# A hybrid decoder step on one core: 72 instead of 64 tokens weighed row by row, in 18 groups six tiles apart, with the two products of a group joined

## The chip, the cores and the metric

The kernel is one program on one core of a Trainium2 chip. The metric is the device time of one execution in microseconds. A profile is one more execution, taken by the hardware profiler; its times are counted from the start of its span. "PE" is TensorE (its weight loads are listed apart as "PEld"), "DVE" is VectorE, "ACT" is ScalarE, "POOL" is GpSimd and "SP" is SyncE, which does nothing here but issue DMAs.

## The reference, cut to what matters

One decoder layer runs on 288 tokens: 256 of a prompt and 8 x 4 of a decode batch. A first half (an input projection, a short gated convolution, sparse attention in three branches, merge gates, an output projection) is followed by an expert mixer, and that is where the change does most of its work:

```
s = einsum('nhcd,hckd->nhck', qq, sub_keys)      # 8 heads, 2 halves, 128 keys
top, sel = top_k(s1 + s2, 16)                    # 16 of 128 x 128 experts per head
g = softmax(top)
a = gelu(einsum('nd,nhkd->nhk', hx, u_tab[eidx]))
y = einsum('nhk,nhkd->nd', g * a, v_tab[eidx])   # 8 x 16 = 128 experts per token
```

`u_tab` and `v_tab` have 16384 rows of 1024 numbers. In the attention half, the cached keys and values of the compressed branch go through a small two-layer network (`compress`: sums over 32 positions, a gelu, a product with `w2`), and the prompt's queries read 15 compressed values each next to the selected and the window values.

## The kernel before

**The expert mixer as dense work.** Both tables are read whole, 512 KB a tile. There are 128 tiles of `u` and 128 tiles of `v`. Every float32 product is made of three products in a reduced form: the weights and the moving operand are each split into a high and a low part (`w_hi`, `w_lo` by ACT and DVE, one pair of buffers each), and high x high, high x low and low x high are summed.

- The *u stage* (`split_tile`, called for `E_U + j`, lines 2119 to 2134) makes the activations of 128 experts for all 288 tokens: 16 matmuls with `w_hi` (line 2128) and 8 with `w_lo` (line 2133) a tile, 288 columns each. ACT applies the gelu. Between tile 71 and tile 94 PE also makes, for four tokens a time, the matrix of gates from two one-hot matrices (`route`, line 2182), which DVE multiplies with the activations.
- The *v stage* (`value_tile`) multiplies each tile with the weighted activations of the `ND` dense tokens. The high and the low part of the moving operand lie side by side, so a tile is 8 matmuls of 2 x ND = 448 columns with `w_hi` (line 2208) and 8 of ND = 224 columns with `w_lo` (line 2215). For every tile ACT and DVE split the weights (lines 957, 1417) and the moving operand (`mov_high`, line 1020, and `mov_low_part`, line 1628).

**The last `NE` = 64 tokens by rows.** They take part in the u stage like the others, but not in the v stage. Each of them needs just 128 rows of `v_tab`. POOL gathers these rows with indirect DMAs: `gather_row(k, q)` (line 596) brings the half rows (512 numbers) of 128 experts for one token, 128 x 512 x 4 bytes, and `gather_value` (line 603) brings a token's 128 activations, 128 x 4 bytes, from a copy in memory (`act_kept`). A *group* is `GRP` = 4 tokens: 8 row gathers and 4 value gathers. A *unit* is one half of a group: `weigh_unit(k)` multiplies the rows of four tokens with their weights, in four matmuls of 512 columns that lie side by side in the array (32 weight columns each, line 2246), in full float32, of which the profile records two matmuls each. It adds into bank 6 for the first halves and into bank 7 for the second halves. There is one buffer of rows for each half.

**The order of the work.** Every queue is written out by hand, with semaphores between the engines. PE makes the first unit of group g before value tile `UNIT_TILES[g]` = 13 + 7g and the second one `LATER` = 3 tiles behind it. POOL refills a half's buffer once PE has used it (`rows_used`), and spreads its gathers over the tiles of the period by waiting for the tile count (`at_tile`). The ring of 4 slots of 512 KB, filled by SP, feeds the tables: a slot is loaded again when DVE has made its low part. All DMAs, SP's and POOL's, run on the same 16 DMA engines of the core.

**The attention half.** `comp_out(u)` is the product with `w2`; for the values of the paged caches it makes four products with 64 rows of output each, and one copy by ACT (line 850) takes the two blocks. `prompt_values(u)` sums, for each of four heads r in turn, one product with 16 rows (the compressed values, line 1977) and then 2 or 4 products with 128 rows (line 1981). It is called four times. The cached keys and values are loaded by POOL and SP with one DMA a page.

Of the kernel before, what the change touches and what calls it, by code (L numbers as in the profile page):

```python
# [20 lines left out]
NH, NG, R = 8, 2, 4  # L21
HD = 64
# [7 lines left out]
P = 128  # L30
# [17 lines left out]
NE = 64  # L48
ND = NT - NE
GROUPS = (ND - P) // GRP  # L50
EGROUPS = NE // GRP
UNIT_TILES = [13 + 7 * g for g in range(EGROUPS)]
LATER = 3
SUM_AT = UNIT_TILES[-1] + LATER + 2
STAGE = 4
# [50 lines left out]
UP0 = 17904  # L106
# [112 lines left out]
def program(nc, A, O):  # L219
    with ExitStack() as ctx:  # L220
# [315 lines left out]
        def _(pool):  # L536
# [81 lines left out]
            def at_unit(g, x):  # L618

                if g + 1 < EGROUPS:  # L620
                    gather_value(g + 1, x)

            for g in range(1, EGROUPS):
                T = UNIT_TILES[g - 1]
                if g >= 2:
                    pool.wait_ge(S["s_weights"], 2 + g - 1)
                pool.wait_ge(S["rows_used"], 2 * (g - 1) + 1)
                gather_row(2 * g, 0)
                at_tile(T + 1)
                gather_row(2 * g, 1)  # L630
                at_unit(g, 0)
                at_tile(T + 2)
                gather_row(2 * g, 2)
                at_unit(g, 1)
                at_tile(T + 3)
                gather_row(2 * g, 3)
                pool.wait_ge(S["rows_used"], 2 * (g - 1) + 2)
                gather_row(2 * g + 1, 0)
                at_unit(g, 2)
                at_tile(T + 5)  # L640
                gather_row(2 * g + 1, 1)
                at_unit(g, 3)
                at_tile(T + 6)
                gather_row(2 * g + 1, 2)
                gather_row(2 * g + 1, 3)


        @block.scalar
        def _(act):
# [162 lines left out]
            for u, (t, v) in enumerate(UNITS):  # L812
# [34 lines left out]
                if v == 0:  # L847
                    act.activation(kcn[0:n, t, :], ps[0:n, 5, 0:P], ACT.Copy).then_inc(S["cmp_copied"], 1)
                elif t < 4:
                    act.activation(vc[0:64, 2 * t:2 * t + 2, :], ps[0:64, 5, 0:256].rearrange("p (b c) -> p b c", b=2), ACT.Copy)\  # L850
                        .then_inc(S["cmp_copied"], 1)
                else:
                    act.activation(vc[0:16, 8, :], ps[0:16, 5, 0:P], ACT.Copy).then_inc(S["cmp_copied"], 1)
# [833 lines left out]
        def _(pe):  # L1687
# [175 lines left out]
            def comp_out(u):  # L1863

                t, v = UNITS[u]
                n = P if t < 4 else 16
                pe.wait_ge(S["hid_ready"], u + 1)
                if u:
                    pe.wait_ge(S["cmp_copied"], u)
                w2 = M("w2")[:, v * HD:(v + 1) * HD]  # L1870
                if v == 0 or t == 4:
                    for g in range(NG):
                        last = pe.matmul(ps[0:n, 5, g * HD:(g + 1) * HD], hid[:, g * n:(g + 1) * n], w2, start=True, stop=True)
                else:
                    for b in range(2):
                        for g in range(NG):
                            last = pe.matmul(ps[0:64, 5, b * P + g * HD:b * P + (g + 1) * HD], hid[:, g * P + b * 64:g * P + b * 64 + 64], w2,
                                             start=True, stop=True)
                last.then_inc(S["comp_out"], 1)
# [86 lines left out]
            def prompt_values(u):  # L1966
# [8 lines left out]
                for r in range(R):  # L1975
                    o = ps[:, 5, r * P:(r + 1) * P]
                    pe.matmul(o, vc[0:16, 8, :], pT[0:16, 2048 + r * P:2048 + (r + 1) * P], start=True, stop=False)
                    for br in range(2):
                        for kt in range(qt + 1):
                            x = (4 * br + r) * (qt + 1) + kt  # L1980
                            last = pe.matmul(o, vnew[:, kt, br * P:(br + 1) * P], pT[:, x * P:(x + 1) * P], start=False,
                                             stop=(br == 1 and kt == qt))
# [277 lines left out]
            for t in range(PK):  # L2260
# [5 lines left out]
                if t - LATER in UNIT_TILES:  # L2266
                    weigh_unit(2 * UNIT_TILES.index(t - LATER) + 1)
# [133 lines left out]
```

## Time and profile before

| | |
|---|---|
| Time, median of 3 runs | 1222.1 us (1221.54 to 1223.38) |
| The profiled execution's own time | 1216.64 us |
| Its span | 1214.9 us |
| PE busy | 1187.8 us, 98% of the span |
| DVE, ACT, POOL busy | 826.3, 614.3, 559.8 us |
| Moved by DMA | 263.67 MB, mean 217 GB/s |
| Granted PE clock, mean | 0.994 |

The profiled execution took 5.5 us less than the median of the runs. Its time goes 1.7 us beyond its span, for what lies before the first and behind the last instruction. A group of instructions in a view is named by its line, its engine, what it writes and reads; "x8" is the count, and a time in square brackets is how long the engine was idle before the group, with what ended it.

### The profile page before, as it was taken

What the parts mean: (1) busy time and instruction counts of PE and PEld (TensorE: products, weight loads), DVE (VectorE), ACT (ScalarE), POOL (GpSimd) and SP (SyncE); (2) the same over time, 40 slices, a digit from 0 to 9 for tenths busy, and PEclk for the clock granted to TensorE, in tenths of its full rate; (3) what the DMA queues carried; (4) which work ended last, traced back from release to release, by engine and by line L of the source; (5) the groups of instructions that cost most, each with busy time, mean ns of one, the idle gap of its engine ahead of it and who ended that gap; (6) DMA issues with size and microseconds to landing.
All of it is one profiled execution on the core that took longest, in us unless ns stands there. A gap on an engine that the chain in (4) does not pass through costs nothing.

```text
span 1214.9 us, 23500 instructions
## 1 busy us (share of the span) xinstructions
PE 1187.8 (98%) x8372; PEld 1091.5 (90%) x8372; DVE 826.3 (68%) x1517; ACT 614.3 (51%) x1181; POOL 559.8 (46%) x525
## 2 busy tenths in 40 slices
PE   7999899999999999999999999999999999999998
PEld 5688898977899999999999999999888888888887
DVE  6445465754686799999946765666766667666666
ACT  5423464532353454554557775444555555555554
POOL 3430234432000387877678775001355556665640
PEclk9999998999999999999999999999999999999999
DMA  8672758867665367777776556777888888788883
GB/s 329 208 216 64 108 162 250 265 209 255 206 234 172 105 182 171 165 177 177 182 176 143 132 144 185 261 257 235 307 274 289 290 291 284 272 297 287 293 293 134
DMA packets 144740, 263.67 MB, mean 217 GB/s; under 512 B 55536, under 2 KB 84272, under 8 KB 143920
## 3 DMA queue, kind: packets, MB, share of 16 engines
q1 hardware_dynamic: 100176, 207.29, 52.2%
q0 software_dynamic: 37184, 51.48, 17.1%
q10 hardware_dynamic: 7264, 3.40, 1.2%
q8 instruction: 67, 1.10, 0.4%
q14 instruction: 49, 0.40, 0.1%
HBM read 246.18 MB, written 20.09 MB: 219 GB/s over the span
## 4 chain that ended last, share of the span: by engine, by line
PE 85%; issue 5%; SPq 2%; POOLq 2%; DMA 2%; DVE 2%; POOL 1%; ACT 1%; ACTq 0%; DVEq 0%
PE ps L2128 26%; PE ps L2208 18%; PE ps L2133 13%; PE ps L2215 9%; PE ps L1692 5%; PE ps L2246 3%; PE ps L2182 2%; PE ps L1838 1%; POOLq L551 1%; PE ps L1712 1%; POOL arena L552 1%; PE ps L1719 1%; DMA xT<-in_xT 1%; DMA arena<-in_cache_cmp_v 1%; PE ps L2158 1%
## 5 line engine op out<-in xcount | busy, mean ns | idle before, releaser
L1417 DVE TENSOR_TENSOR w_lo<-ring,w_hi 128x1024 fp32r<-128x1024 f32 x271 | 331.6, 1224 | 130.5 <-ACT w_hi L957 112.0
L957 ACT ACTIVATE w_hi<-ring 128x1024 fp32r<-128x1024 f32 x280 | 294.9, 1053 | 203.8 <-issue 111.2
L2128 PE MATMUL ps<-h_hi,w_hi 128*128 128x288 f32 x1088 | 296.8, 300 | 0.5 <-ACT w_hi L957 0.5
L2128 PE MATMUL ps<-h_lo,w_hi 128*128 128x288 f32 x1024 | 277.7, 295 | 0.0
L587 POOL DMA_INDIRECT gates<-arena x128 | 237.4, 1855 | 67.2 <-issue 44.3
L2128 PEld LDWEIGHTS ps<-h_hi,w_hi 128*128 128x128 f32 x1088 | 205.0, 188 | 1.2 <-ACT w_hi L957 1.0
L2128 PEld LDWEIGHTS ps<-h_lo,w_hi 128*128 128x128 f32 x1024 | 192.6, 188 | 0.0
L596 POOL DMA_INDIRECT arena<-in_v,aux x128 | 131.4, 1027 | 129.9 <-PE ps L2215 59.2
L2133 PE MATMUL ps<-h_hi,w_lo 128*128 128x288 f32 x1088 | 166.8, 295 | 0.2 <-DVE w_lo L1417 0.2
L2133 PEld LDWEIGHTS ps<-h_hi,w_lo 128*128 128x128 f32 x1088 | 152.0, 188 | 0.5 <-DVE w_lo L1417 0.5
L2208 PE MATMUL ps<-h_hi,w_hi 128*128 128x448 f32 x512 | 118.2, 373 | 3.7 <-issue 2.9
L2208 PE MATMUL ps<-mov,w_hi 128*128 128x448 f32 x512 | 117.0, 370 | 0.6 <-issue 0.5
L2208 PEld LDWEIGHTS ps<-h_hi,w_hi 128*128 128x128 f32 x512 | 92.3, 190 | 23.9 <-issue 17.1
L603 POOL DMA_INDIRECT arena<-act_kept,aux x64 | 61.3, 957 | 111.7 <-DMA act_kept<-arena 92.5
L2208 PEld LDWEIGHTS ps<-mov,w_hi 128*128 128x128 f32 x512 | 91.4, 189 | 20.4 <-issue 14.1
L577 POOL TENSOR_TENSOR w_lo<-ring,w_hi 128x1024 fp32r<-128x1024 f32 x9 | 24.5, 2727 | 127.3 <-ACT w_hi L957 127.2
L1020 ACT ACTIVATE h_hi<-arena 128x448 fp32r<-128x448 f32 x64 | 37.0, 578 | 86.5 <-PE ps L2215 66.3
L1020 ACT ACTIVATE mov<-arena 128x448 fp32r<-128x448 f32 x64 | 37.0, 578 | 83.0 <-PE ps L2215 62.8
L2215 PEld LDWEIGHTS ps<-h_hi,w_lo 128*128 128x128 f32 x512 | 67.4, 192 | 1.9
L1628 DVE TENSOR_TENSOR h_hi<-arena,h_hi 128x448 fp32r<-128x448 f32 x64 | 40.0, 625 | 42.7 <-ACT h_hi L1020 26.3
L2215 PEld LDWEIGHTS ps<-mov,w_lo 128*128 128x128 f32 x512 | 67.1, 191 | 1.9
L1628 DVE TENSOR_TENSOR mov<-arena,mov 128x448 fp32r<-128x448 f32 x64 | 40.0, 626 | 40.5 <-ACT mov L1020 26.5
(361 smaller groups left out, 1975.4 us busy)
## 6 DMA issues: line engine op xcount, KB each, us to landing
ring<-in_uT SPq DMA_DIRECT2D x128, 512.0 KB
ring<-in_v SPq DMA_DIRECT2D x128, 512.0 KB
ring<-in_wout SPq DMA_DIRECT2D x32, 512.0 KB
ring<-in_wT SPq DMA_DIRECT2D x28, 512.0 KB
gates<-aux SPq DMA_DIRECT2D x32, 256.0 KB, 5.9
ring<-in_wtok SPq DMA_DIRECT2D x8, 512.0 KB
arena<-in_cache_slc_v POOLq DMA_DIRECT2D x64, 64.0 KB
act_kept<-arena SPq DMA_DIRECT2D x32, 128.0 KB
```

The costliest lines, as they stand in the source:

```text
L587: pool.indirect_dma_start(gates, bass.IndirectOffsetOnAxis(rt("gi")[:, P + s:P + s + 1].bitcast(U32), 0), rt("gi")[:, s:s + 1], None, comp ...
L596: pool.indirect_dma_start(e_rows[k % 2][:, 512 * q:512 * q + 512], None, A["v"].rearrange("t p (c f) -> (t p c) f", f=512), bass.IndirectO ...
L603: pool.indirect_dma_start(e_act[:, n:n + 1], None, act_kept, bass.IndirectOffsetOnAxis(act_list[:, ND + n:ND + n + 1], 0))\
L957: act.activation(w_hi[e % 2][:, :], ring[:, (W_O + e) % RING, :], ACT.Copy).then_inc(S["w_high"], 1)
L1020: act.activation(mov_parts[t % 2][:, :, 0, :], rows[:, 2 * pp:2 * pp + 2, :], ACT.Copy).then_inc(S["mov_high"], 1)
L1417: dve.tensor_tensor(w_lo[e % 2][:, :], ring[:, (W_O + e) % RING, :], w_hi[e % 2][:, :].bitcast(F32), ALU.subtract)\
L1628: dve.tensor_tensor(mov_parts[t % 2][:, :, 1, :], rows[:, 2 * pp:2 * pp + 2, :], mov_parts[t % 2][:, :, 0, :].bitcast(F32), ALU.subtract)\
L1692: last = pe.matmul(ps[:, bank, 0:NT], ring[:, i % RING, at + k * P:at + (k + 1) * P], rhs[:, k, :], start=(k == 0), stop=(k == n - 1))
L2128: last = pe.matmul(ps[:, bank, 0:NT], w_hi[e % 2][:, k * P:(k + 1) * P], mov[:, k, :], start=(k == 0 and mov is mov_hi), stop=False, skip_ ...
L2133: last = pe.matmul(ps[:, bank, 0:NT], w_lo[e % 2][:, k * P:(k + 1) * P], mov_hi[:, k, :], start=False, stop=(k == KC - 1), skip_group_chec ...
L2208: last = pe.matmul(ps[:, VBANK[dh][m], 0:2 * ND], w_hi[e % 2][:, h * 512 + m * P:h * 512 + (m + 1) * P], both[h], start=(t % HALF == 0 and ...
L2215: last = pe.matmul(ps[:, VBANK[dh][m], 0:ND], w_lo[e % 2][:, h * 512 + m * P:h * 512 + (m + 1) * P], both[h][:, 0:ND], start=False, stop=( ...
```

## The change

Five things change:

1. `NE` goes from 64 to 72 tokens by rows, so `ND` goes from 224 to 216. The dense groups that the route products make go from 24 to 22, the groups by rows from 16 to 18. `UNIT_TILES` is 13 + 6g (13 to 115) in place of 13 + 7g (13 to 118).
2. The two units of a group are made one behind the other, before the same tile; `LATER` is gone.
3. POOL's order in a period is new: both halves' buffers are refilled together. The old order in a period was (r a row gather, v a value gather, T the tile of the group): r, then at T+1 r v, at T+2 r v, at T+3 r, then (second half free) r v, at T+5 r v, at T+6 r r. The new one is r r r, at T+1 r r v, at T+2 r v v, at T+3 r r v.
4. `prompt_values` makes the four 16-row products first, then the others.
5. `comp_out` makes two products for all units, and ACT takes the paged values in two copies of 128 columns.

```diff
-NE = 64
+NE = 72
...
-UNIT_TILES = [13 + 7 * g for g in range(EGROUPS)]
-LATER = 3
-SUM_AT = UNIT_TILES[-1] + LATER + 2
+UNIT_TILES = [13 + 6 * g for g in range(EGROUPS)]
+SUM_AT = UNIT_TILES[-1] + 2
...
                 if g >= 2:
                     pool.wait_ge(S["s_weights"], 2 + g - 1)
-                pool.wait_ge(S["rows_used"], 2 * (g - 1) + 1)
-                gather_row(2 * g, 0)
+                for half in range(2):
+                    pool.wait_ge(S["rows_used"], 2 * (g - 1) + half + 1)
+                    gather_row(2 * g + half, 0)
+                gather_row(2 * g, 1)
                 at_tile(T + 1)
-                gather_row(2 * g, 1)
-                at_unit(g, 0)
+                gather_row(2 * g + 1, 1)
+                gather_row(2 * g, 2)
+                next_value(g, 0)
                 at_tile(T + 2)
-                gather_row(2 * g, 2)
-                at_unit(g, 1)
+                gather_row(2 * g + 1, 2)
+                next_value(g, 1)
+                next_value(g, 2)
                 at_tile(T + 3)
                 gather_row(2 * g, 3)
-                pool.wait_ge(S["rows_used"], 2 * (g - 1) + 2)
-                gather_row(2 * g + 1, 0)
-                at_unit(g, 2)
-                at_tile(T + 5)
-                gather_row(2 * g + 1, 1)
-                at_unit(g, 3)
-                at_tile(T + 6)
-                gather_row(2 * g + 1, 2)
                 gather_row(2 * g + 1, 3)
+                next_value(g, 3)
...
-                    act.activation(vc[0:64, 2 * t:2 * t + 2, :], ps[0:64, 5, 0:256].rearrange("p (b c) -> p b c", b=2), ACT.Copy)\
-                        .then_inc(S["cmp_copied"], 1)
+                    for b in range(2):
+                        last = act.activation(vc[0:64, 2 * t + b, :], ps[64 * b:64 * b + 64, 5, 0:P], ACT.Copy)
+                    last.then_inc(S["cmp_copied"], 1)
...
-                if v == 0 or t == 4:
-                    for g in range(NG):
-                        last = pe.matmul(ps[0:n, 5, g * HD:(g + 1) * HD], hid[:, g * n:(g + 1) * n], w2, start=True, stop=True)
-                else:
-                    for b in range(2):
-                        for g in range(NG):
-                            last = pe.matmul(ps[0:64, 5, b * P + g * HD:b * P + (g + 1) * HD], hid[:, g * P + b * 64:g * P + b * 64 + 64], w2,
-                                             start=True, stop=True)
+                for g in range(NG):
+                    last = pe.matmul(ps[0:n, 5, g * HD:(g + 1) * HD], hid[:, g * n:(g + 1) * n], w2, start=True, stop=True)
...
                 for r in range(R):
                     o = ps[:, 5, r * P:(r + 1) * P]
-                    pe.matmul(o, vc[0:16, 8, :], pT[0:16, 2048 + r * P:2048 + (r + 1) * P], start=True, stop=False)
+                    pe.matmul(o, vc[0:16, 8, :], pT[0:16, 2048 + r * P:2048 + (r + 1) * P], start=(r == 0), stop=False, skip_group_check=True)
+                for r in range(R):
+                    o = ps[:, 5, r * P:(r + 1) * P]
...
                 if t in UNIT_TILES:
                     weigh_unit(2 * UNIT_TILES.index(t))
-                if t - LATER in UNIT_TILES:
-                    weigh_unit(2 * UNIT_TILES.index(t - LATER) + 1)
+                    weigh_unit(2 * UNIT_TILES.index(t) + 1)
```

A place in the arena that depends on `ND` moves too (`UP0` 17904 to 17520).

## Rows read from the trace of the kernel before

**Rows 1.** The page: busy time of each engine, and the chain that ended last by line.
```profile
PE 1187.8 (98%) x8372; PEld 1091.5 (90%) x8372; DVE 826.3 (68%) x1517; ACT 614.3 (51%) x1181; POOL 559.8 (46%) x525
...
PE ps L2128 26%; PE ps L2208 18%; PE ps L2133 13%; PE ps L2215 9%; PE ps L1692 5%; PE ps L2246 3%; PE ps L2182 2%; PE ps L1838 1%; POOLq L551 1%; PE ps L1712 1%; POOL arena L552 1%; PE ps L1719 1%; DMA xT<-in_xT 1%; DMA arena<-in_cache_cmp_
```
**Rows 2.** Windows: a 7-tile period, then 860 to 868; last: clock, DMA share, GB/s.
```profile
960.45:980.46 20.01, 20.01 (x129) 17.24 (x129) 13.04 (x16) 10.70 (x14) 11.64 (x13) 1.00 0.84 290
...
860.00:864.00 4.00, 1.15 (x7) 0.87 (x5) 1.39 (x2) 1.52 (x2) 3.08 (x4) 0.94 0.96 378
864.00:868.00 4.00, 3.97 (x17) 3.50 (x16) 2.07 (x4) 1.89 (x3) 0.02 (x1) 0.64 1.02 408
```
**Rows 3.** The chain in order of time, v stage: start, us, what.
```profile
880.48 1.00 PE ps L2246 x8
881.48 1.84 PE ps L2208 x8
883.32 0.88 PE ps L2215 x8
884.20 1.63 PE ps L2208 x8
...
900.49 0.99 PE ps L2246 x8
```
**Rows 4.** The chain in order of time: matmuls of 512, 256, 34 and 288 columns.
```profile
21.55 1.85 PE ps L1712 x8
...
60.95 6.91 PE ps L1838 x32
...
109.37 3.66 PE ps L1838 x32
...
729.14 2.16 PE ps L2128 x16
...
733.25 2.16 PE ps L2128 x16
...
736.46 2.13 PE ps L2128 x16
```
**Rows 5.** Line 2246, the units: count, durations in ns, first and last start.
```profile
L2246 PE MATMUL ps<-arena x256: 592/605/617, 880.4 to 1191.1; 128*32 128x512 f32 x128
```
**Rows 6.** Timeline of POOL, v stage; in brackets the idle time before.
```profile
962.33 1.16 POOL L596 DMA_INDIRECT arena<-in_v,aux  x1 [1.84 <-PE ps L2246]
...
965.77 0.95 POOL L603 DMA_INDIRECT arena<-act_kept,aux  x1 [0.30 <-issue]
...
971.91 1.00 POOL L596 DMA_INDIRECT arena<-in_v,aux  x1 [1.42 <-PE ps L2246]
...
1060.36 1.40 POOL L596 DMA_INDIRECT arena<-in_v,aux  x1 [0.30 <-issue]
```
**Rows 7.** DMA view: one kind of issue, KB each, median us to landing.
```profile
arena<-in_cache_slc_k POOLq DMA_DIRECT2D x32, 64.0 KB, 3.1
```
**Rows 8.** Waits of POOL: total us, times, longest us.
```profile
POOL gates L587 <- DMA gates<-arena: 22.8, 7, 4.5
```
**Rows 9.** Timeline of PE in prompt_values, and a wait some 40 us behind it.
```profile
208.91 0.48 PE L1977 MATMUL ps<-arena 16*128 16x128 f32 x2
...
209.97 0.48 PE L1977 MATMUL ps<-arena 16*128 16x128 f32 x2
...
250.19 2.76 PE L2017 MATMUL ps<-arena 128*32 128x512 f32 x18 [2.67 <-DMA arena<-in_cache_slc_k]
```
**Rows 10.** The chain in order of time, across that wait and a later one.
```profile
245.15 5.00 DMA arena<-in_cache_slc_k
...
270.02 4.51 DMA arena<-in_cache_win_kT
274.58 3.20 PE ps L2017 x14
```
**Rows 11.** Line 850, ACT's copy of the compressed values: durations in ns.
```profile
L850 ACT ACTIVATE arena<-ps x4: 357/361/378, 151.7 to 170.3; 64x256 f32<-64x256 f32 x4
```

More of the change, by code:

```diff
@@ L104 @@
 assert USED <= ARENA, (USED, ARENA)
-UP0 = 17904
+UP0 = 17520
 RT, USED = columns([("qq", 16 * NT), ("sub", 2048), ("sp", 3 * 2048), ("lv", 256), ("li", 256), ("lf", 256),
@@ L616, in at_tile, with next_value @@
                 pool.wait_ge(S["lo_used"], E_V + t)
-            def at_unit(g, x):
+            def next_value(g, x):
                 if g + 1 < EGROUPS:
@@ L1981, in prompt_values @@
                             last = pe.matmul(o, vnew[:, kt, br * P:(br + 1) * P], pT[:, x * P:(x + 1) * P], start=False,
-                                             stop=(br == 1 and kt == qt))
+                                             stop=(br == 1 and kt == qt), skip_group_check=True)
                 last.then_inc(S["po_mm"], 1)
```

## The prediction

> **What bounds the kernel now.** I read the page first, then the windows, then the chain of waits, then POOL's timeline. The page shows PE busy for 98% of the span, and PE's lines hold nearly the whole chain [rows 1]: a change counts by what it does to PE's queue. In a steady 7-tile period of the v stage PE has no gap, DVE works 13.04 of 20.01 us, ACT 10.70, POOL 11.64, and the 16 DMA engines are 84% busy at 290 GB/s [rows 2]. So PE sets the pace, but DMA has only 16% to spare, and POOL works through a list of gathers that PE waits for if it is late. There is one exception in the attention half: from about 180 to 275 us the chain runs through POOL's and SP's page loads.
>
> **The dense tiles: -7.2 us.** A steady tile is 8 matmuls with w_hi in 1.63 us (204 ns each, 448 columns) and 8 with w_lo in 0.88 us (110 ns, 224 columns), 2.51 us in all [rows 3]. What is a column worth? The same kind of matmul takes 1.85/8 = 231 ns with 512 columns and 2.13/16 = 133 ns with 288 [rows 4]: 0.44 ns a column. On that line 448 columns give 203 ns, as seen, but 224 would give 105 ns, and 110 are seen. And a matmul of 34 columns, in the other format, still takes 3.66/32 = 114 ns behind a full load of 128 weight columns [rows 4]. I read this as a floor of about 110 ns, set by the weight load, on which the w_lo matmuls already lie. Then 16 fewer columns give 16 x 0.44 = 7 ns on each of 128 x 8 = 1024 w_hi matmuls, 7.2 us, and 8 fewer give nothing on the 1024 w_lo ones. If there is no floor, it is 3.6 us more; both ends are kept. A tile becomes 2.46 us. The Trainium skill has both sides of this: "TensorE: Matmul & The Clock Gate", section "LDWEIGHTS (loading the stationary operand)", takes P/1.2 ns for P weight columns, 107 ns for 128, while its section "Back-to-back issue gap" gives N/2.4 + 2.5 ns, 92.5 ns for 216 columns; by the second alone the w_lo matmuls would be far below what the trace shows, so I go with the first. DVE and ACT get 4% shorter pieces in the mov split, which hides under PE anyway.
>
> **The units: -1.3 us.** From one first unit to the next it is 900.49 - 880.48 = 20.01 us [rows 3]; 7 tiles are 17.6, so a unit costs 1.2 us: 1.00 of its own and 0.21 in the tile behind it (1.84 for 1.63). The 256 recorded matmuls [rows 5] are 32 units, 38.6 us. In a joined pair the second half can stream at once. Float32 columns cost 6.91/32/256 = 0.84 ns [rows 4], 512 of them 0.43 us, and a unit is two such rounds (four side by side, two passes): 0.86 us. A pair is then 1.2 + 0.86 = 2.07 us, 18 pairs 37.3 us: -1.3. If joining saves nothing, 18 x 2.41 = 43.4, +4.8 us.
>
> **The route products: -1.8 us.** A u tile with a route product takes 733.25 - 729.14 = 4.11 us, one without 736.46 - 733.25 = 3.21 [rows 4]. Two groups fewer: 2 x 0.9. Nothing else in the u stage changes on PE, as its matmuls keep all 288 columns.
>
> **Whether the rows come in time.** This decides. The natural period is now 6 x 2.46 + 2.07 = 16.8 us. In it POOL must issue 8 row and 4 value gathers and the rows must land. Count from the start U of a pair. POOL's first gather of a period starts 1.87 us behind the unit (962.33; the unit before it starts at 960.45, the window's edge), because two waits lie in front of it, and takes 1.16 [rows 2, 6]. Each other one takes 0.95 with 0.30 before it, 1.25 us [rows 6]. None of the new waits on tiles holds it (tile T ends at U + 4.5, the gather behind that wait is due at 5.9). So the gathers start at 1.9, 3.4, 4.6, 5.9, 7.1, 8.4, ... and the last rows, tenth and eleventh in the list, at 13.4 and 14.65. POOL is busy nearly all of the period: 12 gathers need 15.3 us.
>
> When do they land? The trace gives no landing for these gathers. The nearest rows: POOL's 64 KB loads land 3.1 us after issue (median) [rows 7]; one took 5.0 [rows 10]; and an indirect DMA of POOL's, the scatter at line 587, is waited for 22.8/7 = 3.3 us behind its own 0.95, 4.2 in all [rows 8]. I take 4.2, with 3.1 and 5.0 as ends. The tenth gather (last row of the first half) is then there at U + 17.6, the eleventh at U + 18.85. PE wants the first at U + 16.8 and the second 0.86 later. A wait at the first half delays the anchor of the next period's POOL work, one between the halves only partly (POOL restarts on the first half), so the period is the larger of 17.6 and about (15.95 + 18.85)/2 = 17.4: 17.6 us.
>
> That supposes that POOL never waits for its queue. The trace shows that it does when rows crowd: the third row gather in a close sequence came 1.42 us behind the one before it instead of 0.30 (971.91), and one at 1060.36 took 1.40 for 0.95 [rows 6]. The new order begins with five row gathers in a line. I take half of that delay of 1.1 us, 0.55: a period of 18.1 us. The DMA engines say the same in another way. A period moves 6 x 512 + 8 x 256 KB = 5.24 MB. In 16.8 us that asks for 312 GB/s; at the 290 that they now give [rows 2] it takes 18.1 us. Nothing in the trace forbids more than 290 (408 are seen in 864 to 868 [rows 2]), but 84% busy at 290 makes 312 a share of 90% on average, and rows can only move in part of the period.
>
> PE is thus held up by 18.1 - 16.8 = 1.3 us a period. The first pair has its rows early, as now, and the last has no value gathers before it; 16 periods remain: 16 x 1.3 = +20.8 us.
>
> **The attention half: 0.** In prompt_values a head takes 209.97 - 208.91 = 1.06 us for 6 recorded matmuls that need about 6 x 0.112 = 0.67: 0.39 us go to the two changes between 16 and 128 rows [rows 9]. One pair of changes in place of four saves 3 x 0.39 = 1.2 us a call, 4.7 us in four calls. But three of the calls lie ahead of a 2.67 us wait for a key page that POOL issued at 245.15 [rows 9, 10], on a chain of POOL issues that does not wait for PE, and 3.5 us earlier at the wait is 3.5 us longer waiting. The fourth call lies ahead of the wait that ends at 274.58, for pages that SP issues one after another [rows 10]. So I count 0; if the cover were gone, -4.7. In comp_out, four times, 8 short matmuls become 4 longer ones (nothing on balance at half the weight columns), and ACT's copy of 0.36 us becomes two [rows 11]: +0.2 us each, at most 0.8 on ACT, hidden or passed on; I take +0.2.
>
> **The sum.** -7.2 - 1.3 - 1.8 + 20.8 + 0.2 = +10.7 us. The profiled execution would go from 1216.6 (span 1214.9 and 1.7 around it) to 1227.3. It lies 5.5 us below the median of the runs, and the change adds the same to both: 1222.1 + 10.7 = 1232.8, so 1233 us.
>
> **The rivals.**
>
> *The rows come in time.* It ends on the other side. Speaking for it: the tail of the new order is row, value, value, row, row, so the last rows meet a nearly empty queue, and with a landing in 3.1 us the eleventh is there at U + 17.75 for a need at 17.7. It decides at 10.1/16 = 0.63 us a period: a period below 17.45 us makes the kernel faster. With no wait at all: -7.2 - 1.3 - 1.8 + 0.2 = -10.1, 1212 us (1208 if w_lo has no floor). Against it: 4.2 us for an indirect DMA in the rows, and the crowding. The Trainium skill, "DMA: Bandwidth & Descriptors", section "Anatomy of one DMA — SWDGE (gpsimd) path", fits 2.0 us + bytes/436 GB/s, 2.6 us for these 256 KB; that rule gives this rival's time. No row here shows a POOL DMA as quick. Chance 0.27.
>
> *The queue backs up.* Five rows in a line cost POOL the full 1.1 us or more, landing takes 5.0: the tenth gather is there at U + 13.4 + 1.1 + 5.0 = 19.5, 2.7 us late, 16 times: +43, in all +33, 1255 us. PE's clock adds to it: behind the stall at 860 the granted clock was 0.64 over 4 us, part of it at the lower level [rows 2]. Against it: while PE waits the ring is full and leaves the DMA engines to the rows. Chance 0.15.
>
> *It balances.* Rows late by about 0.6 us a period: 1222 us. Chance 0.08. The forecast, late by 0.8 to 2.2 us: 1225 to 1247, chance 0.50.
>
> **Range and chances.** Both signs hold much of the chance. 1210 to 1252 reaches over the forecast's own range into both rivals and leaves some 2 in 10 out. 0.2%, 2.4 us, is about what a measurement of this kernel can tell from no change. Faster 0.28, same 0.07, slower 0.65.
>
> **What the changed profile would show.** Right: the w_hi group of 8 at 1.57 us, the w_lo group still at 0.88, route products on 22 tiles, pairs of 16 recorded matmuls every 18.1 us, with PE idle before the first or between the halves, released by a gather or by "issue", and POOL without pauses. A period of 16.8 us and no idle time on PE at the pairs would make it wrong, in favour of the first rival; so would w_lo groups of 0.85. If the wait at 250 us is gone instead of longer, the attention half was not covered.

## The result, and the profile after

| | before | after |
|---|---|---|
| Median of the runs beside each other | 1221.8 us (4 runs, 1219.1 to 1223.4) | 1261.1 us (4 runs, 1260.2 to 1266.1) |
| Span of the profiled execution | 1214.9 us | 1258.6 us |
| Mean granted PE clock | 0.994 | 0.975 |

The change makes the kernel slower: 1.0333 times the time before, 95% interval 1.0313 to 1.0352, or +39.3 us. Forecast were +10.7 us and 1210 to 1252. In a second comparison, in another session, the ratio was 1.0325 (1.029 to 1.0359).

The page after: PE's busy time has hardly grown, but its share has fallen, and the last chain is no longer PE's alone [rows 1].

```profile
PE 1194.4 (95%) x8372; PEld 1101.3 (88%) x8372; DVE 822.0 (65%) x1515; ACT 610.7 (49%) x1175; POOL 601.5 (48%) x549
...
PE 66%; DMA 11%; POOL 9%; issue 7%; SPq 2%; POOLq 2%; DVE 1%; ACT 1%; ACTq 0%; DVEq 0%
```

Where the time lies can be read from PE's w_hi line, whose rows give its first and last start. Before the change (line 2208):

```profile
L2208 PE MATMUL ps<-mov,w_hi x512: 358/366/477, 841.9 to 1206.6; 128*128 128x448 f32 x171
L2208 PE MATMUL ps<-h_hi,w_hi x512: 362/366/575, 845.1 to 1209.2; 128*128 128x448 f32 x171
```

After it (line 2201):

```profile
L2201 PE MATMUL ps<-mov,w_hi x512: 352/358/596, 846.3 to 1250.4; 128*128 128x432 f32 x171
L2201 PE MATMUL ps<-h_hi,w_hi x512: 352/360/731, 849.4 to 1252.9; 128*128 128x432 f32 x171
```

The v stage took 1209.2 - 841.9 = 367.3 us, and now takes 1252.9 - 846.3 = 406.6: +39.3 us, all of the difference of the medians. It also begins 4.4 us later in this profile; the first experiment shows that this is not the change's. In the profiles of the kernels below that have the changed first half and 72 tokens it begins anywhere between 840.8 and 846.0 us.

Inside the stage, the chain of waits in order of time, across a pair (lines 2201, 2208 and 2239 are w_hi, w_lo and the units; 595 and 602 the row and the value gathers):

```profile
899.93 5.60 DMA arena<-in_v,aux
...
905.58 1.94 PE ps L2239 x8
907.51 2.41 PE ps L2201 x8
909.92 0.89 PE ps L2208 x8
910.81 0.26 issue
911.07 0.94 POOL arena L595
...
918.58 0.95 POOL arena L595
919.52 0.31 issue
919.83 5.21 DMA arena<-in_v,aux
925.05 0.04 issue
925.09 1.07 PE ps L2239 x8
926.15 1.77 PE ps L2201 x8
927.92 0.88 PE ps L2208 x8
928.81 1.57 PE ps L2201 x8
930.38 0.88 PE ps L2208 x8
```

The chain before was PE, PE, PE [rows 3]. Now each period goes through POOL's list to its last row gather, through that gather's landing (5.60, 5.21), and only then to PE's second unit. In the timeline the first pair starts at 885.17 and the eighteenth at 1218.34: one every (1218.34 - 885.17)/17 = 19.6 us. The dense groups in it are as forecast where nothing disturbs them: 1.57 us with w_hi, 0.88 with w_lo. Right behind a wait they often are not. The w_hi group behind a pair takes 1.76 us when nothing is wrong; in 7 of the 17 periods it takes 2.36 to 3.14, as the 2.41 us at 907.51.

PE's waits in the whole kernel, total, times and longest, and the row of the units:

```profile
PE ps L2239 <- DMA arena<-in_v,aux: 32.8, 29, 2.4
...
L2239 PE MATMUL ps<-arena x288: 592/617/1063, 885.2 to 1220.6; 128*32 128x512 f32 x144
```

Two periods as windows (us, then PE, PEld, DVE, ACT, POOL busy; clock, DMA share, GB/s). They answer to [rows 2]:

```profile
923.01:942.58 19.57, 17.05 (x114) 14.78 (x113) 12.14 (x15) 10.56 (x14) 14.06 (x13) 1.00 0.86 290
961.13:980.83 19.70, 18.56 (x112) 15.49 (x113) 10.25 (x13) 8.01 (x11) 12.32 (x12) 0.91 0.78 255
```

In the second one PE is busy for 1.5 us longer at the same work, at a granted clock of 0.91: part of it ran at 1.2 GHz. POOL, in its timeline, shows what stood in its list [rows 6]:

```profile
924.88 1.82 POOL L595 DMA_INDIRECT arena<-in_v,aux  x1 [1.83 <-PE ps L2239]
927.01 0.95 POOL L595 DMA_INDIRECT arena<-in_v,aux  x1 [0.30 <-issue]
928.26 0.95 POOL L595 DMA_INDIRECT arena<-in_v,aux  x1 [0.30 <-issue]
929.51 1.36 POOL L595 DMA_INDIRECT arena<-in_v,aux  x1 [0.30 <-issue]
931.17 1.26 POOL L595 DMA_INDIRECT arena<-in_v,aux  x1 [0.31 <-issue]
...
937.75 0.95 POOL L595 DMA_INDIRECT arena<-in_v,aux  x1 [0.30 <-issue]
939.00 0.95 POOL L595 DMA_INDIRECT arena<-in_v,aux  x1 [0.30 <-issue]
```

The pair began at 923.01. The first gather is there 1.87 us later, as forecast, but takes 1.82 (the profile shows no reason), and the second one, which must wait until PE has used the second half, starts at 4.0 us where 3.4 was forecast; the last two rows are issued at 14.7 and 16.0 us, where 13.95 and 15.2 were forecast. The 5.60 and 5.21 us of the chain count from the start of such an issue, as the forecast's 4.2 does.

### The profile page after: what moved, and what is told of

Same layout as the page of the kernel before. It is cut to its first block, busy times and chain, and to the rows that moved or that the text cites. A ratio compares the mean times of both kernels' runs of the same rounds, so it can differ in the third digit from the quotient of the medians.

```text
span 1258.6 us, 23516 instructions
## 1 busy us (share of the span) xinstructions
PE 1194.4 (95%) x8372; PEld 1101.3 (88%) x8372; DVE 822.0 (65%) x1515; ACT 610.7 (49%) x1175; POOL 601.5 (48%) x549
## 3 DMA queue, kind: packets, MB, share of 16 engines
q0 software_dynamic: 38720, 55.68, 18.4%
## 4 chain that ended last, share of the span: by engine, by line
PE 66%; DMA 11%; POOL 9%; issue 7%; SPq 2%; POOLq 2%; DVE 1%; ACT 1%; ACTq 0%; DVEq 0%
PE ps L2121 26%; PE ps L2126 13%; DMA arena<-in_v,aux 8%; PE ps L2201 7%; PE ps L1689 5%; POOL arena L595 5%; POOL arena L602 3%; PE ps L2208 3%; PE ps L2239 2%; PE ps L1709 2%; PE ps L2175 2%; PE ps L1835 1%; POOLq L550 1%; POOL arena L551 1%; DMA ring<-in_v 1%
## 5 line engine op out<-in xcount | busy, mean ns | idle before, releaser
L595 POOL DMA_INDIRECT arena<-in_v,aux x144 | 158.0, 1097 | 117.2 <-PE ps L2239 64.0
L2121 PEld LDWEIGHTS ps<-h_hi,w_hi 128*128 128x128 f32 x1088 | 205.3, 189 | 1.2 <-ACT w_hi L954 1.0
L602 POOL DMA_INDIRECT arena<-act_kept,aux x72 | 75.2, 1045 | 114.3 <-DMA act_kept<-arena 92.7
L2201 PE MATMUL ps<-h_hi,w_hi 128*128 128x432 f32 x512 | 120.3, 380 | 3.9 <-ACT w_hi L954 3.3
L2201 PEld LDWEIGHTS ps<-h_hi,w_hi 128*128 128x128 f32 x512 | 97.5, 201 | 26.5 <-issue 18.9
L2201 PE MATMUL ps<-mov,w_hi 128*128 128x432 f32 x512 | 111.8, 360 | 0.6 <-DVE xT L1653 0.6
L1017 ACT ACTIVATE h_hi<-arena 128x432 fp32r<-128x432 f32 x64 | 36.2, 565 | 148.5 <-PE ps L2208 147.5
L1625 DVE TENSOR_TENSOR h_hi<-arena,h_hi 128x432 fp32r<-128x432 f32 x64 | 38.9, 608 | 103.4 <-ACT h_hi L1017 103.4
L2239 PE MATMUL ps<-arena 128*32 128x512 f32 x288 | 42.3, 664 | 32.9 <-DMA arena<-in_v,aux 32.8
L2208 PE MATMUL ps<-h_hi,w_lo 128*128 128x216 f32 x512 | 68.3, 277 | 0.0
```

The source lines that it names most:

```text
L595: pool.indirect_dma_start(e_rows[k % 2][:, 512 * q:512 * q + 512], None, A["v"].rearrange("t p (c f) -> (t p c) f", f=512), bass.IndirectO ...
L602: pool.indirect_dma_start(e_act[:, n:n + 1], None, act_kept, bass.IndirectOffsetOnAxis(act_list[:, ND + n:ND + n + 1], 0))\
L1625: dve.tensor_tensor(mov_parts[t % 2][:, :, 1, :], rows[:, 2 * pp:2 * pp + 2, :], mov_parts[t % 2][:, :, 0, :].bitcast(F32), ALU.subtract)\
L2121: last = pe.matmul(ps[:, bank, 0:NT], w_hi[e % 2][:, k * P:(k + 1) * P], mov[:, k, :], start=(k == 0 and mov is mov_hi), stop=False, skip_ ...
L2201: last = pe.matmul(ps[:, VBANK[dh][m], 0:2 * ND], w_hi[e % 2][:, h * 512 + m * P:h * 512 + (m + 1) * P], both[h], start=(t % HALF == 0 and ...
L2208: last = pe.matmul(ps[:, VBANK[dh][m], 0:ND], w_lo[e % 2][:, h * 512 + m * P:h * 512 + (m + 1) * P], both[h][:, 0:ND], start=False, stop=( ...
```

## The experiments

**1. The attention half alone.** The kernel before with only the edits of `prompt_values` and `comp_out` (its part of the diff as shown ahead).

> The kernel before with only the two edits of the attention half (the 16-row products first, the compressed values in one product with two copies). It tells whether the +4.4 us by which the v stage began later in the profile after belongs to the change. My prediction's step (the saving on PE is eaten by the wait for a key page, ACT's second copy is hidden): 1222, within 1 us of the kernel before. Rival A, the half costs what the two profiles show (u stage 6.2 us later): 1228. Rival B, the 3.5 to 4.7 us saved on PE come through: 1217 to 1218.

Measured: 1220.3 us against 1220.5, ratio 0.9999 (0.9982 to 1.0016). The later start of the v stage was the one execution's: its u stage began late, behind the page loads. The edits do what they say (the 8 recorded short matmuls are one run of 1.15 us where they were four changes [rows 9]), and it is worth nothing. The waits for the key pages in the profile after, against 5.00 and 4.51 us of landing [rows 10]:

```profile
248.66 5.72 DMA arena<-in_cache_slc_k
...
275.83 6.18 DMA arena<-in_cache_win_kT
```

**2. No refill.**

```diff
-            for g in range(1, EGROUPS):
-                T = UNIT_TILES[g - 1]
...
-                pe.wait_ge(S[f"v_in{half}"], 16 * 9 * SETB + 16 * GRP * (g + 1))
+                pe.wait_ge(S[f"v_in{half}"], 16 * 9 * SETB + 16 * GRP)
```

> The kernel after, but POOL gathers rows for the first group only and values for the first two; the later units read the same rows again. Left out: 136 row gathers and 64 value gathers, and with them the right sums of the tokens by rows. PE does all that the kernel after does. Theory, the whole loss is rows that come late: no wait at the pairs, the granted clock stays at 1.0, the time is 1212 (the 10.1 us of the prediction's first three terms), period of a pair 16.8 us. Rival, something else in the change costs time too (the attention half, a slower start of the v stage): 1216 to 1220 with pairs every 16.8 us.

Measured: 1206.8 us, ratio 0.9889 (0.987 to 0.9909), so -13.6 us, 3.5 more than the terms. The weights of the later units are made from the values of the first two groups. Its chain across a pair (lines 2181, 2188, 2219):

```profile
1011.87 1.57 PE ps L2181 x8
1013.44 0.88 PE ps L2188 x8
1014.32 1.85 PE ps L2219 x16
1016.17 1.76 PE ps L2181 x8
```

A pair costs 1.85 + (1.76 - 1.57) = 2.04 us (forecast 2.07), a tile 2.45 (2.46), and the pairs come every 16.76 to 16.78 us (16.8), but for one period of 17.63. So PE's side of the prediction stands, and by the two ratios (1.0333 - 0.9889) 54 us are the rows'. The expected 1212 us was 5 us too high.

**3. Rows of a quarter, two buffers as in the change.**

```diff
-                pool.indirect_dma_start(e_rows[k % 2][:, 512 * q:512 * q + 512], None, A["v"].rearrange("t p (c f) -> (t p c) f", f=512),
+                pool.indirect_dma_start(e_rows[k % 2][:, 512 * q:512 * q + 128], None, A["v"].rearrange("t p (c f) -> (t p c) f", f=128),
```

> The kernel after, but each row gather brings 128 numbers of an expert in place of 512 (64 KB in place of 256 KB a gather; left out: three quarters of each row, so the sums of the tokens by rows are not the reference's). The number of gathers, their order and all waits are the same. Theory A, bytes on the DMA engines make the rows late (a gather lands 5 to 6 us behind its issue, since ring loads and other gathers are before it): landing falls to about 3 us, the eleventh gather is there at 17.7 when it is wanted, waits at the pairs nearly vanish, 1207 to 1214. Theory B, POOL's own list of 12 gathers and the fixed part of a landing are the limit: pairs stay 18 us or more apart, 1230 to 1258.

Measured: 1225.2 us (1220.2 to 1234.6), ratio 1.0059 (1.003 to 1.0088): between the two theories. PE's waits for rows, and three landings from the chain:

```profile
PE ps L2239 <- DMA arena<-in_v,aux: 13.5, 17, 2.9
```

```profile
912.40 3.87 DMA arena<-in_v,aux
930.21 3.43 DMA arena<-in_v,aux
...
1057.86 5.63 DMA arena<-in_v,aux
```

The chain holds one row gather a period, nearly always the last one. With 64 KB they land in 3.4 to 5.6 us, 4.0 in the mean of 16, with 256 KB (17 in the chain of the changed kernel) in 4.3 to 6.8, 5.7 in the mean. So some 1.7 us of the landing are bytes, and with the smaller gathers about 33 of the 54 us go. The other 21 remain with a quarter of the bytes: the last row gather is issued 15.3 to 15.8 us behind most pairs, and with 4.0 us more it is there at 19.3 or later, where the second unit would be due at 17.6. The four longest landings, 4.5 to 5.6 us, lie between 1036 and 1100 us; what made them long is not known.

**4. Filler in the waits.** PE does 272 more recorded matmuls, 17 pairs with 2 x 1 us each.

```diff
+            def filler():
+                for q in range(GRP):
+                    pe.matmul(ps[32 * q:32 * q + 31, 6, :], e_wide[:, 0:31], arena[:, 0:512], start=False, stop=False, skip_group_check=True)
...
+                    for half in range(2):
+                        if g:
+                            filler()
+                        weigh_unit(2 * g + half)
```

> The kernel after with four extra matmuls (31 zero weight columns, 512 columns, added into a sum that they don't change) before each half of a pair but the first, about 1 us each time, 2 us a pair, where PE otherwise waits 1.9 us a pair. The rows come no sooner. Theory, the lower clock behind a wait costs about 12 us (w_hi groups of 1.8 to 3.2 us in place of 1.57 behind the pairs): the waits shrink to near 0 and the granted clock stays at 1.0, 1249 to 1257. Rival, the clock costs little or the pace is set by the rows alone: 1260 to 1268.

Measured: 1249.0 us, ratio 1.0251 (1.0227 to 1.0274): faster than the changed kernel (1.0333) by 10 us, with some 34 us of matmuls more. The first view is that of its waits, the second a window over most of the stage:

```profile
PE ps L2239 <- DMA arena<-in_v,aux: 8.3, 12, 2.1
```

```profile
923.01:1212.00 288.99, 281.88 (x1928) 229.76 (x1928) 169.53 (x204) 137.15 (x182) 181.38 (x174) 1.00 0.81 272
```

The same window of the changed kernel:

```profile
923.01:1212.00 288.99, 258.72 (x1639) 221.11 (x1639) 164.55 (x198) 132.68 (x176) 186.79 (x175) 0.96 0.81 267
```

The granted clock is at 1.00 in place of 0.96, so the part that ran at 1.2 GHz is gone, and the waits have gone from 32.8 to 8.3 us (near 0 was expected). The theory holds: the lower clock behind the waits costs some 10 us.

**5. Joined units at the old density.** The kernel before with 64 tokens and 7 tiles, and POOL's list as in the change.

```diff
-LATER = 3
...
                 if t in UNIT_TILES:
                     weigh_unit(2 * UNIT_TILES.index(t))
-                if t - LATER in UNIT_TILES:
-                    weigh_unit(2 * UNIT_TILES.index(t - LATER) + 1)
+                    weigh_unit(2 * UNIT_TILES.index(t) + 1)
```

> The kernel before (64 tokens, pairs of groups seven tiles apart, old attention half) with the units joined and POOL's list in the new order, nothing else. Its natural period is 7 x 2.51 + 2.0 = 19.6 us, which is also the mean period that the kernel after shows. Theory, the joined order needs about 19.6 us for its rows: few and short waits, the joining saves 16 x 0.3 = 5 us, 1215 to 1222. Rival, the joined order costs time at any spacing, since each wait starts POOL's next list later: 1228 to 1245.

Measured: 1219.2 us against 1218.5, ratio 1.0000 (0.9984 to 1.0016), with 5.5 us in 6 waits. The joined order nearly fits into 19.6 us: about half of the 15 periods last 19.7 us, the mean is 20.2. By the terms joining should have saved some 5 us of PE; with the waits nothing is left of it.

**6. A third buffer for half rows.** There are 2209 free columns behind the two buffers, enough for one more of 2048. Half of a period's gathers are now for a unit one period later.

```diff
-        e_rows = [arena[:, AR_ROWS + i * GRP * 512:AR_ROWS + (i + 1) * GRP * 512] for i in range(2)]
+        e_rows = [arena[:, AR_ROWS + i * GRP * 512:AR_ROWS + (i + 1) * GRP * 512] for i in range(3)]
...
+            pool.wait_ge(S["weighed"], PIECES_IN)
+            for q in range(GRP):
+                gather_row(2, q)
...
+                def row(x):
+                    k = 2 * g + 1 + x // GRP
+                    if x % GRP == 0:
+                        pool.wait_ge(S["rows_used"], k - 2)
+                    if k < 2 * EGROUPS:
+                        gather_row(k, x % GRP)
```

> The kernel after with three buffers of half rows in place of two, so that half of the gathers of a period are for a unit one period later. Bytes, gathers, their spread over the tiles and PE's work are the same; only when a row is due changes. Theory, latency: a row lands 5 to 6 us behind its issue and the last two are issued 13.5 to 16 us into a period of 16.8, but POOL's 12 gathers (15.3 us) and the 16 DMA engines can keep up: no waits at the pairs, 1212 to 1216. Rival, rate: the DMA engines or POOL's queue move 5.24 MB in no less than about 18 us (290 GB/s): pairs every 18 to 19.6 us whatever is due when, 1232 to 1258.

**7. Two units three tiles apart, at 72 tokens and six tiles.** The kernel after with the second unit three tiles behind the first, and the old list squeezed into six tiles.

```diff
+LATER = 3
...
                 at_tile(T + 5)
                 gather_row(2 * g + 1, 1)
                 at_unit(g, 3)
-                at_tile(T + 6)
                 gather_row(2 * g + 1, 2)
                 gather_row(2 * g + 1, 3)
```

> The kernel after, but the two units of a group three tiles apart and POOL's list in the order of before (squeezed from 7 tiles into 6). It tells what the joining costs at the new density. Theory, latency of rows all due at one time: with the halves due at different times each has its own slack, waits nearly vanish, and what is left of the loss of joining is 0.34 us a pair: 1216 to 1222. Rival, density (72 tokens six tiles apart are too many for POOL's list and the queue whatever the order): pairs every 18 us or more, 1235 to 1260.

Measured, both in one session: third_buffer 1242.2 us (1234.4 to 1252.4), ratio 1.0189; split72 1231.7, ratio 1.0091. PE had hardly a wait at the units left (1.4 and 2.4 us), but the periods were long: 16.8 to 24.9 us in third_buffer, half of them 18.3 to 18.7, and 18.4 in the mean in split72. third_buffer thus fell into the range of its rival, split72 between the two. The chain of third_buffer there (lines 2212, 2219; 965 and 1028 are ACT's copies of the weights and of the moving operand):

```profile
1014.79 1.04 ACT w_hi L965
1015.83 4.21 another core or an unknown queue
1020.04 0.02 issue
1020.07 0.04 ACT mov L1028
...
1020.53 1.05 ACT w_hi L965
1021.59 0.04 issue
1021.63 1.82 PE ps L2212 x8
```

I took that for a ceiling of the traffic at about 290 GB/s, which the prediction had also named. Four runs were made to test it: third_buffer with row gathers of 128, of 256, and by turns of 512 and 256 numbers, and with full rows but spread pairs.

```diff
-UNIT_TILES = [13 + 6 * g for g in range(EGROUPS)]
+UNIT_TILES = [13 + 110 * g // 17 for g in range(EGROUPS)]
```

> The kernel with three row buffers, each gather cut to 128 numbers of an expert as in the run of short rows (the same part is left out). With three buffers the pairs had no wait for rows, but PE waited 24 us for ACT's pieces behind them. Theory A, the traffic of 5.24 MB a period is what delays ACT and PE there: with a quarter of the rows' bytes the waits go, 1206 to 1210, pairs 16.8 us apart. Theory B, it is not the bytes but the order of the third-buffer kernel (12 gathers issued without a pause, whatever their size): the waits stay, 1230 to 1245.

> The kernel with three row buffers, each gather cut to 256 numbers of an expert (128 KB; left out: half of each row). A period of 16.76 us then moves 3.15 MB of the table and 1.05 MB of rows, 250 GB/s, where full rows ask for 313. In the profiles with full rows the core moved 283 to 289 GB/s in this stage, whatever the order. Theory, a ceiling of about 290 GB/s for this mix: 250 lies under it, so no waits, 1205 to 1209, as with quarter rows (219 GB/s). Rival, every byte of the rows costs (landing grows with size, with no ceiling): halfway between quarter and full rows, 1220 to 1228.

> The kernel with three row buffers at 72 tokens, with every second gather cut to 256 numbers of an expert (left out: a quarter of the rows' numbers). It asks for 282 GB/s in a period of 16.76 us, and half of its gathers are of full size. Theory (a ceiling that lies between 293 and 313 GB/s): no waits, 1205 to 1210. Rival (the order with three buffers delays PE's partners whenever gathers of full size are among them): some waits, 1215 to 1230.

> The kernel with three row buffers at 72 tokens and full rows, its 18 pairs spread to tile 123 (6.47 tiles apart) in place of 115. The bytes are the same, the mix asks for 306 GB/s in place of 313. Theory, a ceiling of some 290 GB/s on average: the bytes between tile 13 and 123 (95 MB) take 325 to 333 us in either kernel, so spreading gains little, 1228 to 1242. Rival, the loss comes from crowding within a period and falls off fast below 313: 1212 to 1224.

Measured: third_short 1205.5 us (0.9888), third_half 1207.4 (0.9904), third_384 1207.5 (0.9901), third_spread72 1208.2 (0.991, 0.9889 to 0.993). None has a wait at the pairs. The first three move 218 to 281 GB/s and would fit a ceiling as well. The last one decides: it has full rows, and its window shows 307 GB/s and no idle time on PE:

```profile
900.00:1180.00 280.00, 280.00 (x1871) 249.86 (x1863) 189.54 (x225) 152.48 (x203) 204.53 (x184) 1.00 0.90 307
```

So the theory of a ceiling fell, and the first two results became doubtful. Both were repeated in a new session, on another chip, beside the changed kernel:

> The kernel of third_buffer once more, in another session. If the crowding of exact six-tile periods costs the time: 1232 to 1252 again, periods of 18.4 us. If third_buffer's result came from the chip or session it ran on: periods of 16.76 us without waits, as the six-tile periods of third_spread72 have, 1205 to 1210.

> The kernel of split72 once more. If the kernel's order at this density costs the time: 1229 to 1236 again. If the session did: the two halves have a natural period of 17.1 us and POOL's list fits into it, 1208 to 1216.

> The changed kernel once more, beside the other two on the same chip. If its 39 us belong to the kernel: 1256 to 1264, about 1.033 times the kernel before. If they were in part the session's: less, 1235 to 1250.

Measured: third_again 1209.0 us, ratio 0.9921 (0.9905 to 0.9937); split_again 1213.5, ratio 0.9956 (0.9941 to 0.997); after_again 1255.8, ratio 1.0325 (1.029 to 1.0359). Two periods of third_again, whose 17 periods all last 16.76 to 16.78 us but one of 17.64:

```profile
1049.50:1066.27 16.77, 16.77 (x113) 14.88 (x112) 11.08 (x14) 9.09 (x12) 13.11 (x13) 1.00 0.92 316
1066.27:1083.05 16.78, 16.78 (x114) 14.88 (x113) 11.16 (x14) 9.09 (x12) 12.99 (x13) 1.00 0.90 312
```

The changed kernel's loss belongs to it: it shows in both sessions. The 33 and 18 us by which third_buffer and split72 were worse the first time do not belong to these kernels. What they were is open. The view of waits puts them down to "remote" (another core or an unknown queue), on ACT up to 7.8 us long, 57 us in third_buffer and 33 in split72:

```profile
ACT mov L1028 <- remote: 33.8, 12, 4.2
ACT h_hi L1028 <- remote: 23.4, 7, 7.8
```

Neither third_again nor split_again has one. The kernels of experiments 1 and 2 ran in the first session with one such wait of 1.5 us and with none, but they move less. No run separates the session from the chip.

**8. Other ways to give the joined order room,** at fewer tokens: joined64 with its pairs spread to tile 123, the same with 60 tokens, and the same with ten slots for rows in place of eight, used in turn, at 64 and 68 tokens.

```diff
-UNIT_TILES = [13 + 7 * g for g in range(EGROUPS)]
+UNIT_TILES = [13 + 110 * g // 15 for g in range(EGROUPS)]
...
-                pool.indirect_dma_start(e_rows[k % 2][:, 512 * q:512 * q + 512], None
+                pool.indirect_dma_start(e_rows[(4 * k + q) % 10], None
```

> The kernel before with joined units and the new order as in joined64, but the 16 pairs spread to tile 123 in place of 118 (7.33 tiles apart in the mean). The joined order then has 20.3 us for a period where it needs 19.6, and the mix asks for 293 GB/s in place of 297. Theory (the ceiling and the two-buffer order bound it, both just relieved): waits nearly go and the joining's own gain shows, 1212 to 1217. Rival, the joining gains nothing at this traffic: 1218 to 1222.

> 60 tokens by rows in place of 64, 15 pairs spread over tiles 13 to 123 (7.86 apart), joined, new order, two buffers, old attention half. Terms: a tile 228 columns wide (2.53 us), 15 pairs of 1.86, one route product more (0.9); the mix asks for 286 GB/s. Theory, with rows in time and the traffic below 290 the stage takes what PE needs, about 6 us less than before: 1213 to 1217. Rival, fewer tokens by rows only widen the dense tiles: 1219 to 1224.

> As joined64_spread, with ten slots of one token's half rows in place of eight, used in turn, so that two gathers of a period are for the next but one half. If the order of two buffers is what still costs: 1209 to 1213, some 3 us below joined64_spread. If the traffic is: the same as joined64_spread, or worse as with three buffers at 72 tokens.

> ten_slots64 with 68 tokens by rows, 17 pairs spread to tile 123 (6.88 apart); PE needs 2 us less than with 64, the mix asks for 301 GB/s where ten_slots64 asks for 291 and has no wait. If the ceiling lies under 301: 1216 to 1226, with waits for ACT's pieces or for rows. If it lies above: 1208 to 1211.

Measured: joined64_spread 1218.9 us, ratio 0.9981 (0.996 to 1.0003), with 5.4 us of waits left in 5 pairs; joined60 1217.8, 0.9986 (0.9971 to 1.0001); ten_slots64 1212.4, 0.9946 (0.9931 to 0.9962), without a wait at the pairs; ten_slots68 1215.3, 0.9967 (0.9953 to 0.998), with no wait at the pairs in its profile either. Two more slots are worth 6.5 us over the spreading alone. joined64_spread came out where its rival said (1218 to 1222), joined60 and ten_slots68 between their two. Whether 68 tokens are really slower than 64 is not settled: the 3 us are from two sessions, and the intervals of the ratios touch.

## Why the prediction was wrong

Its direction and its place were right, and in the main its mechanism; its size was not: +39.3 us measured, +10.7 forecast. The step that failed is the working of when the rows land: a landing of 4.2 us that was 5.7, and a delay of POOL's list of 0.55 us that was 1.5. The period of 18.1 us that came out of it was 19.6, and its cost of 1.3 us in 16 periods was 2.8 in 17.

- *The dense tiles, -7.2 us; the units, -1.3; the route products, -1.8.* Right, and the sizes too: no_refill shows 1.57, 0.88 and 2.04 us, and the u stage's 128 tiles take 430.9 us before and 429.1 after (409.8 to 840.7 and 416.0 to 845.1 in the rows of its h_lo matmuls), -1.8. The w_lo group did not get shorter with 216 columns (0.88 us), so the floor of 110 ns a matmul is there. That the weight load sets it is inferred, no run varied the weight columns; the Trainium skill, "TensorE: Matmul & The Clock Gate", section "LDWEIGHTS (loading the stationary operand)", gives P/1.2 ns for a load, 107 ns for 128 columns, and the 110 ns agree with that. The v stage of no_refill takes 357.5 us (842.1 to 1199.6) where 367.3 - 8.5 = 358.8 were due. The time of no_refill is 13.6 us below that of the kernel before, 3.5 more than the terms; 1.3 of these are in the v stage, the rest is within the scatter of the single runs (1216.9 to 1228.4 for the kernel before in that session): the spans of the two profiles differ by 9.6 us.
- *The landing, 4.2 us [3.1 to 5.0].* This is the term that was mis-sized. In the changed kernel's chain the gathers land in 4.3 to 6.8 us, 5.7 in the mean of 17, beyond the upper end. The rows that I chose from were of 64 KB loads and of a 4-byte scatter [rows 7, 8], and none had 256 KB in it. short_rows shows that this mattered: at 64 KB the same gathers take 4.0 in the mean, which 4.2 would have fitted. The trace before did have transfers of 256 KB, issued by SP, and they reach from one side of the forecast's range to beyond the other:

```profile
gates<-aux SPq DMA_DIRECT2D x32, 256.0 KB, 5.9
arena<-in_cache_win_kT SPq DMA_DIRECT2D x8, 256.0 KB, 3.4
```

The fit of the Trainium skill, "DMA: Bandwidth & Descriptors", section "Anatomy of one DMA — SWDGE (gpsimd) path", 2.6 us for these bytes, is less than half of what was measured, with table loads on the same engines.
- *POOL's delay, 0.55 us.* It was 1.5 us in the mean (16.1 us for the last row's issue where the count without a delay gave 14.65). Half of it I could have read: the second gather waits for the second half's use, which now is itself late, and starts at 4.1 us in the mean instead of 3.4. The rest is in the waits on tiles, of which the forecast said that none holds the list (some 0.4 us a period: the tiles are late behind a late pair), and in gathers that take up to 2.0 us in place of 0.95. And the 1.42 us at 971.91, which I read as a crowded queue, end with PE's use of the second half [rows 6], a wait that stands in front of that gather in the old list.
- *The period from both.* From one pair's start it is 16.1 + 5.7 = 21.8 us (21.9 without rounding) to the next pair's second unit, which starts 2.3 us behind its first one, because it waits: 19.6, as measured. The forecast had let the tenth gather and the first unit decide; the chain goes through the eleventh and the second unit in 16 of 17 periods. Above 16.76 that makes 2.84 us in each of 17 periods, 48 us, against 1.3 x 16 = 20.8.
- *The clock.* The forecast's sum had nothing for it; it stood only in the rival of the backed-up queue. Of the 48 us PE waited 32.8. Of the other 15, second units that start by themselves are 17 x 0.34 = 6 us (an estimate: 2.41 us for two single units by the rows of before, 2.07 for a pair), and some 10 are left for the same matmuls done slower behind the waits. filler got 10 us back.
- *DMA engines at 290 GB/s, so 18.1 us.* This second argument, which seemed to confirm the first, was wrong: third_again moves 312 to 316 GB/s at a share of 0.90 to 0.92, with 16 of 17 periods at 16.8 us. A rate seen where nothing asked for more is no limit.
- *The attention half, 0.* Right: 0.9999. PE's waits for the key pages grew from 2.7 to 5.4 us, as the prediction had it, if by less than the saving of 4.7.
- *The rivals.* "The queue backs up" (+33, 1255 us, chance 0.15) was the nearest, with the right sign of both its parts: a landing of 5 us or more, and the clock. "The rows come in time" (1212) is what the third buffer makes true: 1209. "It balances" (1222) came nowhere near.

Which edit costs the time? At 72 tokens six tiles apart, split units give 1213.5 us, joined ones with two buffers 1255.8 to 1261, joined ones with three 1209. At 64 tokens seven tiles apart, joined ones with two buffers cost nothing (joined64, 1.0000). So neither the density nor the joining costs the time by itself; the two together do. When joined, all eight gathers of a period are due at one moment and can start only at the pair before: POOL's list (16 us) and a landing (5.7 us) stand in one line, which 19.6 us nearly hold and 16.8 do not. Split halves, or a third buffer, let one landing lie beside the next list. The best version found is the kernel after with three buffers, at six tiles (1209.0, 0.9921) or spread to tile 123 (1208.2, 0.991).

## What to carry to other kernels

When work is joined so that its inputs are due at one time, add up the whole round: release, the list that issues the transfers, the last landing. If that is longer than the period, smaller transfers help only in part (21 of 54 us stayed here with a quarter of the bytes), but one more buffer removes the loss. Price a transfer by its own size and company: rows of transfers four times smaller gave 1.5 us too little here, and 17 periods multiply that. And waits of 1 to 2 us on TensorE cost more than their own length here (33 us of waits, some 10 more in slower matmuls), so put a term for the slower matmuls behind them into the sum.

## What the runs showed of the hardware that was not expected

- Matmuls put into the waits made the kernel faster: some 34 us more of PE work, 10 us less time, with the granted clock at 1.00 where it was 0.96 over the same 289 us. The longest wait for rows in the changed kernel was 2.4 us.
- The 16 DMA engines moved 312 to 316 GB/s over periods of 16.77 us, a mix of 512 KB table loads and POOL's gathers of 2 KB pieces, with no wait on PE.
- The same two kernels took 1242 and 1232 us in one session and 1209 and 1213.5 in another, while the kernel before stayed at 1220.5 and 1219.2. The sessions ran on different chips. On these two kernels a single session's comparison misled by 33 and 18 us; both ask for over 300 GB/s. att_only and no_refill, which ask for less, showed nothing unusual in that session.
